# A gather of 32 tokens by four ranks in place of one token by 128 ranks, in the expert layer of a hybrid decoder step

## The reference

```python
def peer_block(xc, w_query, sub_keys, expert_u, expert_v):
    C = xc.shape[0]
    qh = (xc @ w_query).reshape(C, PEER_HEADS, 2, PEER_HALF)          # 8 heads
    scores = jnp.einsum('chpe,hpne->chpn', qh, sub_keys)
    s, ix = lax.top_k(scores, PEER_TOPK)                              # 16
    ... # 16 x 16 candidates per head, the best 16 of them: eid, softmax gates g
    u = expert_u[eid]                                                 # 128 rows of 1024 floats per token
    act = jax.nn.gelu(jnp.einsum('cd,ced->ce', xc, u))
    return jnp.einsum('ce,ced->cd', (g * act), expert_v[eid])
```

## Time and profile before

| | |
|---|---|
| median of 3 runs (lowest, highest) | 3555.37 us (3552.96, 3562.03) |
| the profiled execution's own time | 3554.18 us |
| its span in the trace | 3552.4 us |
| granted TensorE clock, mean | 0.757 of 2.4 GHz |
| expert rows gathered | 1107.43 MB in 2112 indirect DMAs |

### The profile page before, as it was taken

The page is one execution under the profiler, slowest core; times in us unless marked ns, Lnnn a source line. Parts: engine busy times, 40 slices in busy tenths (PEclk is TensorE's granted clock), DMA queues, the critical chain, the costliest instruction groups (busy, mean ns, idle before and its releaser), DMA issues.

```text
span 3552.4 us, 32315 instructions
## 1 busy us (share of the span) xinstructions
PE 2321.5 (65%) x10360; PEld 787.6 (22%) x10360; DVE 2102.8 (59%) x5353; ACT 498.3 (14%) x824; POOL 2080.6 (59%) x2142
## 2 busy tenths in 40 slices
PE   5989468746987777555967557456654665476553
PEld 2444112213542233111312012001100110011000
DVE  5244798874565666423566747645764575467542
ACT  2462101102221333111210000000000000000000
POOL 0200367774666565524565777776777677777773
PEclk9989678867998777666978678667856776687566
DMA  3342399999999999999999999999999999999996
GB/s 109 135 155 86 126 369 405 405 401 344 408 388 364 381 360 335 395 370 349 399 395 407 406 399 406 405 403 394 404 401 403 397 402 403 404 393 405 397 409 224
DMA packets 361045, 1255.90 MB, mean 354 GB/s; under 512 B 46170, under 2 KB 64986, under 8 KB 356524
## 3 DMA queue, kind: packets, MB, share of 16 engines
q0 software_dynamic: 304128, 1107.43, 80.0%
q1 hardware_dynamic: 56748, 146.41, 11.4%
HBM read 1221.55 MB, written 32.12 MB: 353 GB/s over the span
## 4 chain that ended last, share of the span: by engine, by line
DMA 29%; PE 24%; DVE 12%; POOL 12%; issue 10%; ACT 2%; DVEq 0%; ACTq 0%; SPq 0%; POOLq 0%
DMA v_rows<-expert_v,idx_v 26%; PE y_acc L1905 11%; POOL v_rows L1823 8%; DVE u_rows L1953 4%; POOL u_rows L1811 3%; PE pair L586 3%; PE xb L1886 2%; PE pair L1552 2%; PE pair L2080 1%; PE pair L606 1%; DMA arena<-cache_v_old 1%; DMA arena<-cache_kT 1%; PE pair L996 1%; PE pair L1017 1%; PE pair L1004 1%
## 5 line engine op out<-in xcount | busy, mean ns | idle before, releaser
L1953 DVE CUSTOM_DVE_ANT_0 u_rows<-u_rows,xb 128x1024 f32<-128x1024 f32 x1056 | 1262.9, 1215 | 1085.5 <-PE xb L1886 1059.2
L1811 POOL DMA_INDIRECT u_rows<-expert_u,idx_u x1056 | 1024.7, 970 | 620.3 <-DVE dots L1953 320.6
L1823 POOL DMA_INDIRECT v_rows<-expert_v,idx_v x1056 | 1012.2, 959 | 467.3 <-issue 298.0
L1905 PE MATMUL y_acc<-v_rows,w_row 128*32 128x512 f32 x4224 | 800.1, 897 | 521.2 <-DMA v_rows<-expert_v,idx_v 521.1
L1886 PE MATMUL xb<-parts,pick 48*128 48x512 bf16 x2112 | 482.3, 465 | 368.6 <-DVE dots L1953 368.2
L1905 PEld LDWEIGHTS y_acc<-v_rows,w_row 128*32 128x32 f32 x4224 | 145.4, 142 | 904.8 <-issue 469.8
L2080 PE MATMUL pair<-arena 128*128 128x512 f32 x576 | 318.6, 654 | 13.6 <-PEq L66 13.6
L1886 PEld LDWEIGHTS xb<-parts,pick 48*128 48x128 bf16 x2112 | 97.6, 97 | 999.0 <-DVE dots L1953 601.5
L1920 ACT ACTIVATE acts<-dots 128x16 f32<-128x16 f32 x66 | 14.2, 216 | 1352.9 <-DVE dots L1953 1333.5
L586 PE MATMUL pair<-arena 128*128 128x272 f32 (+1 forms) x576 | 159.2, 431 | 2.6 <-DVEq L757 1.7
L1793 POOL MEMSET pick<- 128x2048 bf16 x1 | 1.8, 1804 | 227.4 <-POOLq L66 227.4
(11 more groups left out here) (299 smaller groups left out, 2153.5 us busy)
## 6 DMA issues: line engine op xcount, KB each, us to landing
u_rows<-expert_u,idx_u POOLq DMA_INDIRECT x1056, 12.7
v_rows<-expert_v,idx_v POOLq DMA_INDIRECT x1056
arena<-w_in_tiles SPq DMA_DIRECT2D x32, 512.0 KB, 4.1
arena<-w_query_by_group SPq DMA_DIRECT2D x8, 2048.0 KB, 20.4
arena<-cache_kT SPq DMA_DIRECT2D x8, 1792.0 KB, 16.9
arena<-cache_v_near SPq DMA_DIRECT2D x8, 1024.0 KB, 9.6
parts<-x_parts SPq DMA_DIRECT2D x132, 48.0 KB, 5.4
arena<-x_prompt SPq DMA_DIRECT2D x12, 512.0 KB, 6.8
```

The costliest lines, as they stand in the source:

```text
L1811: nc.gpsimd.indirect_dma_start(self.u_rows[:, n % U_SLOTS, :], None, a["expert_u"][0], bass.IndirectOffsetOnAxis(ap=self.idx_u[(b + 1) % 2 ...
L1823: nc.gpsimd.indirect_dma_start(self.v_rows[:, n % V_SLOTS, :], None, a["expert_v"][0], bass.IndirectOffsetOnAxis(ap=self.idx_v[b % 2][:, a ...
L1905: last = nc.tensor.matmul(self.acc[g * BAND:(g + 1) * BAND, half:half + HALF], self.w_row[:, b % 2, lo:lo + BAND], self.v_rows[:, (TB * b ...
L1953: nc.vector.tensor_tensor_reduce(out=self.u_rows[:, n % U_SLOTS, :], in0=self.u_rows[:, n % U_SLOTS, :], in1=self.xb[:, n % XB_SLOTS, :], ...
```

## The change

**The gather.** The i-th gather of a block of 32 tokens now takes ranks 4i to 4i + 3 of all 32 tokens (partition 32 k + c holds rank 4i + k of token c). The number of gathers, their size and their slots are the same, and `n` now counts gathers.

**x.** `xb` holds the 32 tokens' x four times over the partitions and serves 32 gathers: PE makes it with two fp32 matmuls from a tile of x in fp32 (`repeat_x`), 33 times in all. `merge` stores x once in fp32 (`x_norm`) and no bf16 pieces; SP loads 9 tiles in place of 132 pieces of 48 KB.

**The sum.** Each gather's weights are spread to 128x32 (`w_sel`, one DVE product per 16 gathers). `combine` has the same eight matmuls for 4 gathers, now per 32 tokens; then ACT copies `acc` (`take_sums`), PE adds its four bands with two matmuls (`add_bands`), ACT copies the 32 rows (`keep_rows`), 33 times in all.

**The router.** Gates and numbers are made per group g of two heads, spread with `selx` on PE and copied by ACT with eight small copies (`act_spread`), so a group's eight gathers per block can start before the later groups are found. The gathers read their row numbers straight from `idx`; the copies to `idx_u` and `idx_v` are gone. ALONG_STEPS is 40 (36), and tile 0's remaining router steps are paced over the first OPENING = 18 gathers.

```diff
+ALONG_STEPS = 40
+OPENING = 18
+SPREAD = {max(ASKED, FIND + VSTEPS * (g + 1)): g for g in range(NG)}
 def pool_to(self, pool, upto):
-                if t == 0:
-                    pool.wait_ge(self.idx_u_ready, b + 2)
+                if n % P < BAND and n % 8 == 0:
+                    pool.wait_ge(self.kept, NG * (n // P) + n % P // 8 + 1)
                 if n >= U_SLOTS:
                     pool.wait_ge(self.dot_done, n - U_SLOTS + 1)
+def repeat_x(self, pe, k):
+        pe.wait_ge(self.xn_landed, 16 * (tile + 1))
+        if k >= 2:
+            pe.wait_ge(self.dot_done, BAND * (k - 1))
+            pe.wait_ge(self.y_kept, k - 1)
+        for half in range(0, D, HALF):
+            last = self.nc.tensor.matmul(self.xb[:, k % 2, half:half + HALF], self.c.selx[0:rows, block, :],
+                                         self.xn[0:rows, half:half + HALF], start=True, stop=True)
 def pe_to(self, pe, upto):
-                if n >= XB_SLOTS:
-                    pe.wait_ge(self.dot_done, n - XB_SLOTS + 1)
-                for half in range(2):
-                    last = nc.tensor.matmul(self.xb[:, n % XB_SLOTS, ...], self.pick[rows, t, :], self.parts[...])
+            if b >= BB and b % BB == 0 and t == 4:
+                self.add_bands(pe, b // BB - 1)
+            if ub % BB == BB - 1 and t == TB - 4 and ub // BB + 1 < NTOK // BAND:
+                self.repeat_x(pe, ub // BB + 1)
+def take_sums(self, act, k):
+        act.wait_ge(self.v_free, BAND * (k + 1))
+        for half in range(0, D, HALF):
+            self.nc.scalar.activation(self.sums[:, half:half + HALF], self.acc[:, half:half + HALF], ACT.Copy)
 def dve_to(self, dve, upto):
+                if n % BAND == 0:
+                    dve.wait_ge(self.xb_ready, n // BAND + 1)
                 dve.wait_ge(self.u_landed[n % U_SLOTS], 16 * (n // U_SLOTS + 1))
-                dve.wait_ge(self.xb_ready, n + 1)
-                    self.indices(self.idx_v, b + 1).then_inc(self.idx_v_ready, 1)
-                    self.indices(self.idx_u, b + 2).then_inc(self.idx_u_ready, 1)
+                nc.vector.tensor_tensor(self.w_sel[:, ub % 2], self.c.rep[:]..., self.share[:]..., ALU.mult)
 def early_pace(r):
             if r == 0:
-                return Still()
+                return Pace(tok, 0, OPENING, [0] * ASKED + [1] * (RSTEPS - ASKED))
```

More of the change, by code:

```diff
@@ L1727 @@
 TB = 16
+BAND = 32
+GROUPS = 4
+BB = BAND // TB
 QB = P // TB
[L1729 to L1731 removed]
 NB = NTOK // TB
@@ L1872, in pe_to @@
     def pe_to(self, pe, upto):
-        nc = self.nc
         for b, t in self.span("pe", upto):
-            if b + 1 < NB:
-                n = TB * (b + 1) + t
-                sub = n // SUB
-                if n == 0:
-                    pe.wait_ge(self.const_ready, 8)
-                if n % SUB == 0:
-                    pe.wait_ge(self.parts_landed[sub % PARTS], 32 * (sub // PARTS + 1))
-                if n >= XB_SLOTS:
-                    pe.wait_ge(self.dot_done, n - XB_SLOTS + 1)
-                for half in range(2):
-                    rows = slice(64 * half, 64 * half + 3 * SUB)
-                    last = nc.tensor.matmul(self.xb[:, n % XB_SLOTS, half * HALF:(half + 1) * HALF], self.pick[rows, t, :],
-                                            self.parts[rows, sub % PARTS, :], start=True, stop=True)
-                last.then_inc(self.xb_ready, 1)
+            ub = b + 1
@@ L1909, in combine, with add_bands @@
         last.then_inc(self.v_free, GROUPS)
+    def add_bands(self, pe, k):
+        block = k % (P // BAND)
+        pe.wait_ge(self.dot_done, BAND * (k + 1))
+        for half in range(0, D, HALF):
+            pe.wait_ge(self.acc_read, 2 * k + half // HALF + 1)
+            last = self.nc.tensor.matmul(self.xb[block * BAND:(block + 1) * BAND, k % 2, half:half + HALF], self.c.rep[:],
+                                         self.sums[:, half:half + HALF], start=True, stop=True)
+        last.then_inc(self.y_summed, 1)
```

418 lines of the change are left out of this document (206 added, 212 removed).

## The result

The changed kernel takes 3404.34 us (median of 4 runs, 3401.41 to 3405.69), the kernel before 3554.16 us in the same job (4 runs, 3551.76 to 3562.03). The ratio is 0.9574, with a 95% interval of 0.9557 to 0.959: 150 us or 4.3% faster. The profiled execution of after took 3404.3 us, its span is 3402.1 us.

The account below looks back on a forecast made before the run. DMA transfers were taken to bound 2000 us (480 to 800, 1800 to 3480). From 3554.2, minus 26 (opening), 33 (middle), 15 (other transfers) and 5 (tail), came 3475, put at 3476 for the median; range 3445 to 3525.

Parts of the forecast that it names:

- The step that failed: All gathers: 1.315 us each, 2777 us for 2112, unchanged in number and size by the change.
- dearer-gather rival: All gathers: rows from 32 tokens cost more; 3615 us if 5% dearer; chance 0.06.
- repeats of x (middle): 800 to 1800 us: dots no longer wait for PE's xb per gather, winning two thirds of 50 us, 33 us.
- other transfers: Main block: small loads and late stores fall away, rows of 4 KB are added; net gain 15 us.
- new work of sum, weights, router, and the loads of x in fp32: Beside the gathers: added PE, DVE and ACT work stays covered by the transfers, at no cost.
- early start: Opening: first gather at 385 instead of 420.9, effective start 402 instead of 428; gain 26 us, bounds 0 and 36.
- tail: After the last u gathers: 8 us gained, about 3 us of added steps; net gain 5 us.
- The opening: Start of the gathers: first u gather at 385, 18 dots done by about 441, gain 26 us.
- the bound of 50: 800 to 1800 us: the most the middle could gain, from a DMA share of 0.98 against 1.03.
- the first rival: 800 to 1800 us: the middle's loss stays, v becoming late in place of u; 3509 us, chance 0.22.
- The low clock: 800 to 1800 us: PE, with less work, falls to the low clock; 3540 us, chance 0.05.
- still 76 or 77: Undisturbed stretch of 200 us: the count of u gathers stays as before; fewer than 75 would mean dearer gathers.

Follow-up runs that it names:

- e10: The changed kernel with 128 unused bytes in front of u_rows and v_rows, both starting 384 past a multiple of 512: 3449.55 us.
- e7: The changed kernel plus unread loads, two of 48 rows of 1 KB per 16 gathers: 3449.96 us.
- e2: The kernel before with xb made once per 16 tokens instead of once per token: 3489.24 us.
- e6: The kernel before with xb made once per 16 tokens and without 124 of 132 loads of pieces: 3455.73 us.
- e12: The kernel of e6 with 384 unused bytes in front of the slots, both starting 256 past a multiple of 512: 3397.39 us.
- e4: The changed kernel with each gather taking one token's 128 ranks again, so without the early start: 3414.96 us.
- e16: The kernel of e2 with 384 unused bytes in front of the slots, both starting 256 past a multiple of 512: 3457.16 us.
- e8: The changed kernel plus unread loads, two of 16 rows of 4 KB per 16 gathers: 3477.26 us.
- e1: The kernel before with each row number XORed with 129 times its partition, so other rows are gathered: 3556.69 us, ratio 1.0.
- e11: The changed kernel with 256 unused bytes in front of the slots, both starting at a multiple of 512: 3397.06 us.
- e14: The changed kernel with 128 unused bytes between u_rows and v_rows, starting 256 and 384 past a multiple of 512: 3399.85 us.
- e17: The changed kernel with u_rows and the gates' tile swapped; u_rows starts 128, v_rows 256 past a multiple of 512: 3402.80 us.
- e13: The changed kernel with 384 unused bytes in front of the slots, both starting 128 past a multiple of 512: 3448.74 us.
- e15: The changed kernel with 64 unused bytes in front of the slots, both starting 320 past a multiple of 512: 3449.36 us.
- e9: The kernel before with 384 unused bytes in front of the slots, both starting 256 past a multiple of 512: 3527.43 us.

## Why the prediction was wrong

**The step that failed** is in the first paragraph of the prediction: "1.315 us for one ... and the change doesn't alter their number or size", on the ground that a share of 1.02 to 1.03 means a stretch bound by transfers. The price of 1.315 us was that of a layout, not of a gather. The change shifted `u_rows` and `v_rows` from 384 to 256 past a multiple of 512, by way of the tiles allocated ahead of them (`selx`, `rep`, `idx` and the gates in place of `idxT` and `gateT`), and the rows then came at POOL's 1.25 us. With the rows put back to 384 (e10) the same changed kernel takes 3449.55 us: 26 below the forecast, but inside its range. The other terms were off by up to 35 us in both directions and partly cancel, so that this lies inside is in part luck. The diff shows the new tiles, but no part of the prediction looked at addresses, although the page of the Trainium skill that it cites for packets has the rule on starts at multiples of 256 bytes (above). The dearer-gather rival looked at the right quantity with the wrong sign and the wrong cause. The premise under all of it, that a share of 1.02 to 1.03 means engines that can't move more, is what e7's two stretches refute.

The terms, each by the pair of kernels that measures it, from before to after (each beside those above it, so another order could split them otherwise):

| term | forecast | measured | from |
|---|---|---|---|
| repeats of x (middle) | -33 | -68 | e2 - before |
| other transfers | -15 | -34, loads of pieces alone | e6 - e2 |
| place of the slots | 0 | -58 (-45 between e10 and after) | e12 - e6 |
| new work of sum, weights, router, and the loads of x in fp32 | 0 | +18 | e4 - e12 |
| early start | -26 | -11 | after - e4 |
| tail | -5 | 0, within those above | traces |

The first five are steps of one chain, so they add up to what separates before and after whatever their sizes: -153 with the 3557.21 us that before took beside e2 (the 150 us above are against 3554.16).

- *The opening.* First u gather 385.1 as forecast (385), and 18 dots done by 440.8 where 441 was forecast (with 1.15 us for a dot, where the earlier trace rows has 1.22). Right as a timeline, but the early start gives 11 us of the 26. Counted in gathers issued by 480, before has 40, e4 (no early start) 52 and after 60. After is then 20 gathers ahead of before, 26 us at 1.315, as forecast; but 12 of them e4 has too, and the early start's own 8 are 10 us at 1.25. In its extra time POOL waits, up to 480, 8 us for the later groups' row numbers and 15 us for dots. From 480 to 800 after has 394 GB/s and e4 401, with DVE 93% busy in both (297 of 320 us, 291 forecast), so DVE's load doesn't explain that difference.
- *The middle.* e2 shows that removing the per-token repeats is worth 68 us, twice my 33 and more than the bound of 50. The bound was made from the share (1.03 - 0.98), and in the earlier trace rows the bytes say more: 371 GB/s against 403 are 8% of 1000 us, 79 us. The share counted engines as busy that moved less. Part of the middle's loss stayed, as the first rival said (v slots, 121 us of waits).
- *Other transfers.* The mechanism is there, mis-sized: the loads of pieces cost 34 us at the old place, and at the new one 60 (e16 - e12), or 46 (e7 - after). The forecast was net of what is added; the 9 loads of x in fp32 (4.3 MB, by bytes some 10 us at 417 GB/s, an estimate) stand in the row of the new work. On the rule of the Trainium skill that was weighed (DMA: Bandwidth & Descriptors, Specifications, 512 B as the smallest transfer at line rate): e8's rows of 4 KB cost more than e7's of 1 KB, so short packets aren't the price here, but the bytes alone (16 us of e7's 46) aren't either. How a pair of small loads drags the gathers down for 200 us stays open.
- *The tail.* From the last u gather to the end of the last combine: 48.8 us (3328.16 to 3376.94), before 52.6 (3478.86 to 3531.50), so 4 us gained where 8 were forecast. The added steps `take_sums`, `add_bands`, `keep_rows` took 5.4 us rather than 3. From the last u gather to the end of the span it is 73.9 us, before 73.5: no gain.
- *The other rivals.* The low clock didn't come: the granted clock of 800 to 1800 is 0.80 (0.79 before). The price of the rows' order is nil (e1, e4).
- *The new work.* e4 moves 392 GB/s in 1200 to 1800 and e12 403, where the stages' PE and DVE work is dense (first e4, then e12). I had set it at nothing under the cover of the transfers. Which of its parts costs the 18 us isn't shown.

```profile
1200.00:1800.00 600.00, 383.49 (x2102) 154.41 (x2098) 323.76 (x688) 150.86 (x230) 343.71 (x354) 0.76 1.01 392
1200.00:1800.00 600.00, 351.63 (x1947) 137.88 (x1948) 312.30 (x660) 129.03 (x195) 340.24 (x348) 0.74 1.02 403
```

The count "still 76 or 77" u gathers in 200 us, named ahead as the test, read 78 in after (78 to 80 in later stretches): a miss in the direction that the prediction had not provided for.

## What to carry to other kernels

Where a stretch is called bound by transfers, check it by bytes per us against the issuing engine's own period and the waits for slots, and not by the share of busy DMA engines: it read 1.02 to 1.03 here at 378, 409 and 420 GB/s. Look at where the big DMA targets start in SBUF before and after any change that allocates in front of them; a pad of 128 bytes is one line and moved this kernel by 45 us, and e11 (starts at multiples of 512) is as fast as the changed kernel or 7 us faster, their intervals overlap. A price taken from a trace is the price in that layout.

## What the runs showed of the hardware

- Two arrays that gathers of 4 KB rows fill in turn: 417 to 420 GB/s in 2200 to 2400 when at least one starts at a multiple of 256 bytes in the partition (after, e11, e12, e14, e17; no small loads beside them), 408 to 410 when both start 64 or 128 off one (320, 384 and 128 past a multiple of 512; e10, e13, e15), at one and the same DMA share. With both off 57 to 70% of the packets took 160 to 172 ns in place of 159; with one off 2%.
- POOL issues an indirect DMA of 128 rows in 0.94 to 0.95 us and 0.30 us between two, so 1.25 us or 419 GB/s for rows of 4 KB; now and then one takes up to 1.9 us.
- Two loads of 48 KB from SP per 16 gathers (6.5 MB in all, 16 us by their bytes) cost 46 us; two of 64 KB in rows of 4 KB (8.7 MB, 21 us) cost 73 us. They bring stretches of 378 to 381 GB/s at an unchanged share of 1.03 (e7, e9).
- Which of a table's rows a gather reads, in which order over the partitions, made no difference (e1: ratio 1.0, 0.9991 to 1.001; e4: 420 GB/s as after).
